# The head-pair stage of a two-block transformer kernel: projections placed between the scores and the value products, and 960 bytes ahead of the second stage's buffers

## The reference, cut to what matters

```python
proj = (rms_norm(x, norm_g) * (1 + scale) + shift) @ w_in
# per head (8 heads, 128 wide), HGRN2:
f = lb + (1 - lb) * sigmoid(hf);  k = 1 - f;  q = silu(hq);  b = cumsum(log f)
A[t,s] = sum_d q[t,d] * exp(b[t,d] - b[s,d]) * k[s,d]      # s <= t
oA = A @ hi
# per head, retention: rotated q, k, decayed scores S[t,s] for s <= t
oB = S @ rv
m = sigmoid(ga) * rms(oA) * silu(hz) + sigmoid(gb) * rms(oB) * silu(rz)
x = x + gate * (m @ w_out)
```

## Time and profile before

| | us |
|---|---|
| median of 3 runs (1857.0 to 1858.25) | 1858.03 |
| profiled execution, its own time | 1858.48 |
| its span, first to last instruction | 1856.3 |
| PE busy | 1737.4 (94%) |
| DVE busy | 848.1 (46%) |
| ACT busy | 766.4 (41%) |
| POOL busy | 675.1 (36%) |

### The profile page before, as it was taken

The page is one execution under the profiler, slowest core; times in us unless marked ns, Lnnn a source line. Parts: engine busy times, 40 slices in busy tenths (PEclk is TensorE's granted clock), DMA queues, the critical chain, the costliest instruction groups (busy, mean ns, idle before and its releaser), DMA issues.

```text
span 1856.3 us, 22400 instructions
## 1 busy us (share of the span) xinstructions
PE 1737.4 (94%) x8181; PEld 1413.9 (76%) x8181; DVE 848.1 (46%) x1342; ACT 766.4 (41%) x1187; POOL 675.1 (36%) x281
## 2 busy tenths in 40 slices
PE   4879988988997999999899999999999999999997
PEld 2767876776785767886688888888888788888885
DVE  7783375376358243998432122124455322122123
ACT  4533544443552356464544222224555453132223
POOL 3342323333233243431344444445311444444442
PEclk7989988988998999999899999999999999999999
DMA  8221321222122134620122322323210223233221
GB/s 335 80 99 49 102 69 62 68 97 68 56 79 102 45 115 75 176 90 0 57 93 99 100 92 90 102 90 114 80 46 35 91 91 102 92 101 101 92 92 67
DMA packets 49876, 166.84 MB, mean 90 GB/s; under 512 B 4987, under 2 KB 9628, under 8 KB 49308
## 3 DMA queue, kind: packets, MB, share of 16 engines
q1 hardware_dynamic: 43696, 153.74, 24.5%
q10 hardware_dynamic: 6124, 12.33, 2.9%
HBM read 160.81 MB, written 5.24 MB: 89 GB/s over the span
## 4 chain that ended last, share of the span: by engine, by line
PE 61%; DVE 4%; ACT 3%; issue 1%; POOL 0%; ACTq 0%; DVEq 0%; POOLq 0%
PE gps L1342 17%; PE gps L1344 17%; PE gps L1343 17%; ACT scores L814 1%; PE gps L1632 1%; PE gps L1558 1%; PE gps L1560 1%; PE gps L1559 1%; PE aps L1612 1%; PE aps L1480 1%; DVE scores L1285 1%; PE aps L1380 0%; PE aps L1622 0%; PE gps L1354 0%; DVE scores L1299 0%
## 5 line engine op out<-in xcount | busy, mean ns | idle before, releaser
L413 POOL TENSOR_TENSOR w_lo<-w_raw,w_hi 128x1024 fp32r<-128x1024 f32 x260 | 647.5, 2494 | 1085.7 <-ACT w_hi L477 1085.7
L1342 PE MATMUL gps<-xa_hi,w_hi 128*128 128x512 f32 x1152 | 461.4, 401 | 20.9 <-POOL xa_lo L420 13.0
L1344 PE MATMUL gps<-xa_hi,w_lo 128*128 128x512 f32 x1152 | 452.4, 393 | 0.0
L1343 PE MATMUL gps<-xa_lo,w_hi 128*128 128x512 f32 x1152 | 452.2, 393 | 0.0
L477 ACT CAST w_hi<-w_raw 128x1024 fp32r<-128x1024 f32 x260 | 270.5, 1043 | 196.7 <-PE gps L1344 135.2
L1342 PE MATMUL gps<-xb_hi,w_hi 128*128 128x512 f32 x736 | 291.5, 396 | 2.6 <-DVE xb_lo L1304 1.4
L1344 PE MATMUL gps<-xb_hi,w_lo 128*128 128x512 f32 x736 | 288.4, 392 | 0.0
L1343 PE MATMUL gps<-xb_lo,w_hi 128*128 128x512 f32 x736 | 286.8, 390 | 0.0
L1342 PEld LDWEIGHTS gps<-xa_hi,w_hi 128*128 128x128 f32 x1152 | 219.1, 190 | 74.0 <-issue 17.8
L1343 PEld LDWEIGHTS gps<-xa_lo,w_hi 128*128 128x128 f32 x1152 | 219.1, 190 | 47.2 <-issue 3.1
L1344 PEld LDWEIGHTS gps<-xa_hi,w_lo 128*128 128x128 f32 x1152 | 218.3, 189 | 46.4
(11 more groups left out here) (248 smaller groups left out, 2096.9 us busy)
## 6 DMA issues: line engine op xcount, KB each, us to landing
w_raw<-weights_dram SPq DMA_DIRECT2D x268, 512.0 KB, 3.3
ada_w<-ada_in_dram SPq DMA_DIRECT2D x8, 1024.0 KB, 16.5
gates<-ret_tab_dram ACTq DMA_DIRECT2D x4, 1024.0 KB, 6.4
rel_scratch_dram<-rel_rows ACTq DMA_DIRECT2D x1, 3072.0 KB, 34.5
x<-xT_dram SPq DMA_DIRECT2D x2, 1024.0 KB, 10.6
res<-xT_dram ACTq DMA_DIRECT2D x1, 2048.0 KB, 8.5
bias<-rel_scratch_dram ACTq DMA_DIRECT2D x1, 2048.0 KB, 10.7
outT_dram<-y SPq DMA_DIRECT2D x8, 256.0 KB, 2.1
```

The costliest lines, as they stand in the source:

```text
L413: TT(w_lo[:, j, :], w_raw[:, j, :], w_hi[:, j, :].bitcast(F32), ALU.subtract).then_inc(lo_ready[j], 1)
L1342: mm(gps[:, j, :], w_hi[:, j, w], x[0][:, k, :], start=k == 0, stop=False)
L1343: mm(gps[:, j, :], w_hi[:, j, w], x[1][:, k, :], start=False, stop=False)
L1344: last = mm(gps[:, j, :], w_lo[:, j, w], x[0][:, k, :], start=False, stop=k == blocks - 1)
```

## The change

It does two things.

1. In the head-pair stage the parts of head 0 are put in another order on three engines, and two helpers are cut in two (`near_scores` into `near_levels` and `near_eye`, `hgrn_scores` into `hgrn_levels` and `hgrn_rest`). On PE chunks 10 and 11 come between the levels and the diagonal, and `ret_scores(0)` between chunks 12 and 13. On DVE the two reductions of chunks 8 and 9 stand ahead of `decayed(0)`; the diagonal of head 0 is copied after the rotation and `exponents(1)`; and `causal(0)` stands ahead of `decayed(1)`. On ACT `values(10, 1)` stands ahead of `far_scores(0)`, and `decays(1)` after the `w_high` of chunk 14. PE waits, before it gives back the slots of chunks 8 and 9, until the values of chunks 4 and 5 are copied. Head 1 keeps its order. No arithmetic is added or taken away.
2. An unused tile of 960 bytes a partition, `line_up`, is allocated ahead of the buffers of `second`. `xb_hi` then begins at byte 118912, which is 128 past a multiple of 1024, as are `xb_lo` and `res`; all others of `second` move by 960 bytes too.

```diff
+XB_PAD = 240
         second = ExitStack()
+        sb("line_up", [P, XB_PAD], where=second)
...
 # ACT
                 ahead(at(9), 1)
+                values(10, 1)
                 far_scores(0)
                 ahead(at(10), 2)
+                ahead(at(11), 3)
                 decays(1)
-                values(10, 1)
-                ahead(at(11), 3)
...
 # DVE
-                def near_scores(e):
+                def near_levels(e):
...
-                    u += len(LEVEL_BANKS)
+
+                def near_eye(e):
+                    u = U_LV[e] + len(LEVEL_BANKS)
...
                 exponents(0)
                 for e in range(2):
-                    was_evicted(2 + e)
-                decayed(0)
-
-                for e in range(2):
                     c = GATE_CHUNKS[e]
...
                     TT(mod[:, bass.ds(p * 2 + (2 * KC + e), 1)], gate_sum[:, e:e + 1], vdyn("b_ada", p * 2 + (2 * KC + e)),
                        ALU.add)
-                near_scores(0)
+                for e in range(2):
+                    was_evicted(2 + e)
+                decayed(0)
+                near_levels(0)
                 for e in range(2):
                     was_evicted(4 + e)
                     dve.sem_inc(evicted[e], 1)
...
                 dve.wait_ge(rot_ready, p * 2 + 2)
+                exponents(1)
+                near_eye(0)
+                causal(0)
                 bank(U_LV[0] + 6)
-                exponents(1)
                 decayed(1)
-                causal(0)
                 z_gate(12, 0, 0, "hg_norm_g")
...
-                near_scores(1)
+                near_levels(1)
+                near_eye(1)
...
 # PE
-                hgrn_scores(0)
+                hgrn_levels(0)
                 for c in GATE_CHUNKS:
 
+                    pe.wait_ge(evicted[c % SLOTS], at(c - 4) + 2)
                     pe.sem_inc(tile_done[c % SLOTS], 1)
                 dense_tokens(at(10), 2, xa)
+                hgrn_rest(0)
                 feature(12)
+                ret_scores(0)
                 feature(13)
-                ret_scores(0)
                 attend(0, 0)
...
-                hgrn_scores(1)
+                hgrn_levels(1)
+                hgrn_rest(1)
```

More of the change, by code:

```diff
@@ L1426, in was_taken, with hgrn_levels @@
                     pe.wait_ge(taken[u % 4], p * USES[u % 4] + (u // 4 + 2))
-                def hgrn_scores(e):
+                def hgrn_levels(e):
                     u = U_LV[e]
@@ L1441, in hgrn_scores, with hgrn_rest @@
                         last.then_inc(bank_full[(u + n) % 4], 1)
-                    u += len(LEVEL_BANKS)
+                def hgrn_rest(e):
+                    u = U_LV[e] + len(LEVEL_BANKS)
                     b = bank(u)
```

## The result

The changed kernel takes 1779.61 us (median of 4 runs, 1779.29 to 1783.42) where the kernel before took 1858.14 (4 runs, 1857.0 to 1858.55): a ratio of 0.9583, 95% interval 0.9566 to 0.9600. The forecast was 1779.5. The profiled execution lasted 1779.5 us, its span 1777.7, at a mean granted clock of 0.987 (0.965 before).

The account below looks back on a forecast made before the run. PE, busy 94% of the span, was taken as the bound. Waits 56.1 plus slow matmuls 19.9 less new gap 2.4, plus alignment 4.9, gave 78.5 us off 1858.48: 1780.0, or 1779.5 for the median; range 1774 to 1795.

Parts of the forecast that it names:

- Both stops go: PE's waits in each head pair, at the diagonal (23.9 us) and first scores-by-values product (32.2), vanish: 56.1 us.
- The matmuls behind the stops, 19.9 us: PE's matmuls after both stops, slowed by the clock falling to 1.2 GHz, regain 19.9 us over four pairs.
- A new gap of 0.6 us: PE waits ahead of chunks 10 and 11 for POOL's remainder of chunk 11: 0.6 us a pair, 2.4 in all.
- The reductions are hidden and all behind them is 3.55 us earlier: DVE's two reductions fit into its 4.40 us wait for the exponentials; masked copies and later work come 3.55 us earlier.
- The second stop, and `decayed(1)` hidden: `causal(0)` ends before PE's product needs it, removing 7.7 us plus 2.85 behind; `decayed(1)`, by 597.8, delays nothing.
- The alignment, 4.9 us: Moving `xb` by 960 bytes makes its 736 matmul triples as fast as those on `xa`: 4.9 us.
- the convolution 0: The convolution's 279 matmuls gain nothing from the moved addresses: 0 us, possibly 0.6 either way.
- The sum, 78.5 of 78.5: Whole kernel: a stall part of 73.6 us plus 4.9 for the address of `xb`, 78.5 us saved.
- The clock rival: In the pairs, the new or another short gap still drops PE's clock: about 1801 us; chance 0.09.
- The slower rival: PE without rests loses its clock in the pair stage: 1910 us if for half of it; chance 0.02.

Follow-up runs that it names:

- late_reductions: The changed kernel with DVE's reductions of chunks 8 and 9 put back behind `decayed(0)`: 1781.34 us, ratio 0.9587 to the kernel before.
- pad_only: The kernel before with only the 960-byte tile added, its order untouched: 1854.22 us, ratio 0.9976.
- order_only: The changed kernel without the 960-byte tile: 1783.43 us, ratio 0.9598 to the kernel before.
- early_eleven: The changed kernel with only chunk 11 rounded on ACT ahead of the copies of chunk 7: 1778.73 us, ratio 0.9565 to the kernel before.
- early_rounding: The changed kernel with ACT rounding chunks 10 and 11 ahead of its copies of chunks 6 and 7: 1805.28 us, ratio 0.9717 to the kernel before.

## Why the prediction was right, step by step

- *Both stops go.* Right: neither is in PE's list. The experiments give each its cause: PE's order removes the first; the second doesn't go without `causal(0)` ahead of `decayed(1)`. Whether it also needs PE's scores to be early wasn't run.
- *The matmuls behind the stops, 19.9 us.* Right, pair by pair. The pairs lost 73.9 us; less the 56.1 of waits and with 2.1 of new gaps that makes 19.9. A pair's gain, less its two waits and with its new gap, is 4.1, 4.8, 5.4 and 5.7 us, against 4.1, 4.8, 5.5 and 5.5.
- *A new gap of 0.6 us.* It is 0.53, 2.1 us in all against 2.4.
- *The reductions are hidden and all behind them is 3.55 us earlier.* They are hidden, but this step had a fault that cost nothing: I noted that two increments bring chunks 12 and 13 early and didn't follow them to POOL. The remainder of chunk 12 hit another `q_far` product, so the masked copies began at 506.70, which is 561.24 on the old axis, 2.3 us later than forecast. The rotation, for which I had counted interference, then had none (0.69 us for its first row, not 2.49) and gave it back: it was done by 515.9, the diagonal's copy at 521.99 (576.5), against a need at 578.5. Nor did the time come from this step: `late_reductions`, without it, has pairs as short.
- *The second stop, and `decayed(1)` hidden.* Right. The triangle product is done at 525.9 and needed at 530.90; `decayed(1)` ends at 540.7, 595.2 on the old axis, where 597.8 was the bound. No wait for chunk 16's slot is in the list.
- *The alignment, 4.9 us.* Right in size and cause: 0.0064 us a triple x 736 = 4.7 by the matmuls' distances, and 5.0 by the intervals; `pad_only` and `order_only` give 3.9 net of what follows here. What was missing is the other side: the matmuls that hold `xb` as weights and stream the weights (keys and values of the attention) go from 0.113 to 0.120 us, and the attention's stage is 0.5 us longer. For the convolution 0 was right: 64.8 us before and after.
- *The sum, 78.5 of 78.5.* Its two large terms were right, but that the whole came out to a tenth of a us is luck. Four things that it doesn't have happen to cancel: +0.5 in the prologue, +1.2 in the output projection, +0.5 in the attention, and -2.2 in the first 192 matmuls of the first network, where the granted clock came back sooner. Windows of 43 us from the start of that network, before and after:

```profile
887.70:930.70 43.00, 42.96 (x157) 31.81 (x158) 18.48 (x28) 23.46 (x34) 14.34 (x6) 0.85 0.22 71
814.90:857.90 43.00, 41.49 (x166) 31.46 (x167) 18.51 (x28) 23.92 (x34) 15.99 (x7) 0.94 0.23 74
```

  These 192 matmuls last 51.1 us before and 49.0 after, with operands and addresses unchanged. In the other twelve traces they last 49.0 to 50.7: `pad_only`, with the order of before, 49.7, and `early_eleven`, in the changed order, 50.5. In the same way the output projection's stretch is 57.5 before and in `pad_only`, 58.7 after, 58.8 in `early_eleven`, and 55.9 to 57.5 in the rest. So neither follows the change in any way that these runs show: traces of kernels that are alike in the stretch differ by as much.
- *The clock rival* (0.09) did not decide in the profiled execution, but the argument against it was weak: I set one gap of 1.16 us that left the clock alone against it. `early_rounding` has the clock fall with gaps of 0.98 and 0.66, and the very gap that I forecast at 0.6 dropped it in 4 of the 18 cases in which it was 0.66 to 0.72. One such drop cost 1.5 us, though, not the 5.5 a pair that the rival feared.
- *The slower rival*, a clock that doesn't hold without rests, is refuted: 1.00 in all pairs with PE busy for over 99%.

## What to carry to other kernels

A stop of the bounding engine costs its length and what its clock loses behind it. Here 7.6 us more of waiting cost 16.3, in four stops of 2.4; 31.8 more cost 43; and 4.5 more cost 25.7, in eight gaps below a microsecond. So count short gaps too. When two moves are aimed at the same wait, measure each without the other: here one of them was worth nothing beside the other. Follow every increment that is moved to the last engine that it sets going: two surprises of this case were a POOL instruction that came to lie beside a DVE one. And when a sum comes out to a tenth of a per cent, add it up by stage all the same: here four small terms that nobody forecast cancel.

## What the runs showed of the hardware

- Matmuls of 512 columns, each with its own load of weights, start 0.227 us apart when streamed tile and weights stand 0, 256 or 512 bytes apart (modulo 1024), 0.229 at 64, 0.233 at 128 and 0.2336 at 32. With the weights streamed and `xb` held, 256 columns, it is 0.120 at 0, 256 and 512, 0.113 at 64, 0.1186 at 128 and 0.118 at 32: level isn't the best there. The runs are those of the table above.
- PE's granted clock fell behind gaps as short as 0.69 us, but not always: two gaps of 0.90 to 0.99 and 0.66 to 0.74 within the levels were followed by it in all four pairs of `early_rounding`, one of 0.66 to 0.72 ahead of the tokens in 4 cases of 18, one of 0.53 to 0.55 in none of 18, and 1.16 ahead of a product fed from `xb` was not.
- A DVE instruction with two SBUF operands that meets POOL's remainder (2.4 us, two SBUF operands) ends about 2.2 us later: 2.44 to 4.64 for `qt`, 0.28 to 2.47 and 2.48 for `q_far`. The Trainium skill ("SBUF — State Buffer", section "Who interferes with whom") says that a DVE instruction with two SBUF inputs contends with a GpSimd instruction that reads SBUF. The trace agrees by these rows; the size is this case's.
